# Second input projection: three weight tiles in one piece instead of split, and the first sample's attention four slots later

## What is computed

```python
proj = jnp.einsum('btd,dn->btn', x, w_in)          # x (tokens, 1024), w_in (1024, columns)
q_c, k_c, v_c, g_c, q_d, k_d, v_d, a_d, g_d = jnp.split(proj, ...)
# samples: 32 pages of 128 cached rows, 8 heads of 64
z = jnp.einsum('bqhd,bkhd->bhqk', qblk, kf) + bf
log_1mb = jnp.where(causal, jax.nn.log_sigmoid(-z), 0.0)
suffix = lax.cumsum(log_1mb, axis=3, reverse=True)
excl = jnp.concatenate([suffix[..., 1:], jnp.zeros_like(suffix[..., :1])], axis=-1)
att = jnp.where(causal, jnp.exp(jax.nn.log_sigmoid(z) + excl), 0.0)
out = jnp.einsum('bhqk,bkhd->bqhd', att, vf)
```

## Time and profile before

| | us |
|---|---|
| median of 3 runs (lowest to highest) | 4384.45 (4380.44 to 4393.51) |
| the profiled execution, its span | 4400.05, 4398.3 |
| PE busy in the span | 3311.5 (75%) |
| DVE, ACT, POOL busy | 2270.3, 1114.8, 876.9 |
| mean granted TensorE clock | 0.867 of 2.4 GHz |

### The profile page before, as it was taken

One profiled execution on the slowest core, in us unless ns is written; L12 is line 12 of the kernel. 1 busy time (PEld: TensorE's weight loads), 2 busy tenths in 40 slices (PEclk: granted clock), 3 DMA queues, 4 the chain that ended last, 5 costly groups with the idle time before them and its releaser, 6 DMA issues. The chain is left out here.

```text
span 4398.3 us, 80744 instructions
## 1 busy us (share of the span) xinstructions
PE 3311.5 (75%) x31326; PEld 2805.6 (64%) x31326; DVE 2270.3 (52%) x3271; ACT 1114.8 (25%) x2113; POOL 876.9 (20%) x724
## 2 busy tenths in 40 slices
PE   8799998999922068746968999979777877254279
PEld 6799998999921057725857777758555555153167
DVE  2456664444444942225554766421387777412466
ACT  0045552222213011121000110100276767210400
POOL 4100002222202411002222111022254555000021
PEclk9999999999966566678988999989899999676689
DMA  3445552232223000044554999843301100332343
GB/s 134 149 130 151 149 152 60 47 60 48 47 83 145 0 5 0 0 166 164 177 183 154 325 318 335 281 153 96 102 1 49 49 11 1 132 77 65 129 167 107
DMA packets 435128, 506.29 MB, mean 115 GB/s; under 512 B 179825, under 2 KB 328962, under 8 KB 423370
## 3 DMA queue, kind: packets, MB, share of 16 engines
q1 hardware_dynamic: 318202, 350.22, 25.6%
q10 hardware_dynamic: 116048, 147.59, 10.0%
q0 software_dynamic: 576, 4.21, 0.2%
HBM read 355.56 MB, written 146.36 MB: 114 GB/s over the span
## 5 line engine op out<-in xcount | busy, mean ns | idle before, releaser
L2235 POOL TENSOR_TENSOR sp_att<-sp_beta,sp_left 128x512 f32<-128x512 f32 (+3 forms) x320 | 303.7, 957 | 316.1 <-DVE sp_left L2191 307.2
L102 PE MATMUL po_acc<-po_x_high,po_w_low 128*128 128x412 f32 (+1 forms) x840 | 310.1, 369 | 54.5 <-POOL po_w_low L95 35.7
L102 PE MATMUL pe_acc<-pe_x_high,pe_w_low 128*128 128x412 f32 (+1 forms) x840 | 304.4, 362 | 22.0 <-DVE pe_x_low L95 13.7
L1094 POOL TENSOR_TENSOR rc_ct<-rc_m,rc_lev 128x256 f32<-128x256 f32 x160 | 123.3, 806 | 923.5 <-DVE rc_m L1050 923.5
L103 PE MATMUL po_acc<-po_x_low,po_w_high 128*128 128x412 f32 (+1 forms) x840 | 301.5, 359 | 0.0
L104 PE MATMUL po_acc<-po_x_high,po_w_high 128*128 128x412 f32 (+1 forms) x840 | 300.2, 357 | 0.0
L104 PE MATMUL pe_acc<-pe_x_high,pe_w_high 128*128 128x412 f32 (+1 forms) x840 | 295.3, 352 | 0.0
L103 PE MATMUL pe_acc<-pe_x_low,pe_w_high 128*128 128x412 f32 (+1 forms) x840 | 295.1, 351 | 0.0
L2191 DVE TENSOR_TENSOR_SCAN sp_left<-sp_z,sp_left,sp_zero 128x512 f32<-128x512 f32 x192 | 235.6, 1268 | 97.5 <-ACT sp_z L2135 97.5
L2081 PE MATMUL sp_t<-sp_id,sp_att 128*128 128x128 f32 x1088 | 180.3, 288 | 121.2 <-DVE sp_aT L2197 112.5
L2081 PEld LDWEIGHTS sp_t<-sp_id,sp_att 128*128 128x128 f32 x1088 | 118.2, 144 | 186.1 <-issue 182.6
(11 more groups left out here) (442 smaller groups left out, 8146.2 us busy)
## 6 DMA issues: line engine op xcount, KB each, us to landing
po_work<-in_cache_k SPq DMA_DIRECT2D x256, 256.0 KB, 4.9
po_work<-in_cache_v ACTq DMA_DIRECT2D x256, 256.0 KB, 4.8
scratch_ops<-pe_work SPq DMA_DIRECT2D x160, 128.0 KB, 2.1
rc_opx<-scratch_ops SPq DMA_DIRECT2D x32, 640.0 KB, 8.0
out_z<-pe_o SPq DMA_DIRECT2D x84, 206.0 KB, 2.7
out_z<-po_o ACTq DMA_DIRECT2D x84, 206.0 KB, 4.3
po_w<-in_w_o ACTq DMA_DIRECT2D x23, 512.0 KB, 5.2
pe_w<-in_w_e SPq DMA_DIRECT2D x21, 512.0 KB, 6.3
```

Of the source, the lines that this page charges most:

```text
L102: pe.matmul(out, ll, rh, start=start, stop=False)
L1094: pool.tensor_tensor(ct[q][:, n], m4[q][:, :, 0, :], every(lev[:, n + 1, :]), ALU.mult).then_inc(sem["ct"][q], 1)
L2235: pool.tensor_tensor(att[h][:, n % 3, 0:w], be[h][:, n % 4, 0:w], left[h][tile(n) % 2][:, at + 1:at + 1 + w], ALU.mult).then_inc(at_ok[h], 1)
```

## The change

The order of the groups is changed: tiles 0 and 1 come whole (slots 0 to 9), then block 4 of tile 2 (slot 10), then tile 3 with its last block first (slots 11 to 15), then the other four blocks of tile 2 (slots 16 to 19). From slot 20 on the tiles are as before. There are 22 groups instead of 24. START is 16 instead of 12, and with it every step of the samples stands four slots later; Q_AT follows from the new order and is 13 instead of 9.

```diff
-ODD_GROUPS = ([(0, range(NBLK))] + [(n, [NBLK - 1]) for n in (1, 2, 3)] + [(n, range(NBLK - 1)) for n in (1, 2, 3)]
-              + [(n, range(NBLK)) for n in range(4, 21)])
+ODD_GROUPS = ([(0, range(NBLK)), (1, range(NBLK)), (2, [NBLK - 1]), (3, [NBLK - 1, *range(NBLK - 1)]),
+               (2, range(NBLK - 1))] + [(n, range(NBLK)) for n in range(4, 21)])
@@
-        START, PER = 12, 10
+        START, PER = 16, 10
```

## The result

The changed kernel takes 4371.98 us (median of 22 runs, 4339.45 to 4387.84), the kernel before in the same comparison 4383.03 (22 runs, 4363.24 to 4437.59). The ratio is 0.9961 with a 95% interval of 0.9942 to 0.9980: 0.4% faster, 9 to 25 us. A second comparison of the same changed kernel gave 0.9944 (0.9918 to 0.9971), 13 to 36 us. A copy of the kernel before gave 1.0033 (1.0004 to 1.0061) against itself, so these intervals are too narrow, and the runs alone hardly tell a gain of 0.4% from chance.

A forecast was written before the change was run, and what follows sets the result against it. PE's own idle time was taken to bound the stage, chiefly waits for split weights and attention weights. Terms of 5.2 + 5.4 + 5 + 9.3 = 24.9 us less took 4384.45 to 4360, range 4346 to 4377.

The forecast's parts named there:

- The early slots: PE from slot 5 to slot 20: fewer waits for split weights, so slot 20 starts 23.1 us earlier.
- START: All sample steps on PE and ACT stand four slots later, 17.9 us, so the first exponential comes 5.2 us earlier.
- my margin of 4.6 us: Ahead of ACT's first exponential: DVE's bias for the first sample ends 4.6 us before ACT wants it.
- The attention weights: PE's seven waits for `po_att`, now in slots without a weight request: 5.4 us less, ends 0 and 15.0.
- only the slots: Rival, 25 in 100: the wait for `po_att` doesn't shrink, a V page or bandwidth being late; 14.5 us left, 4370.
- The clock: Behind the `po_att` waits: shorter idle time loses the clock less often, 5 us less, ends 0 and 12.
- The tail: From slot 101 to the stage's end, four V groups following slot 104: 9.3 us shorter, 7.2 to 10.4.
- The sum: All terms together: 5.2 (first sample) + 5.4 + 5 + 9.3 = 24.9 us less.
- the likeliest case: The forecast itself with all its terms, 53 in 100: 4360 us, own range 4349 to 4368.
- The slower rival, K's pages behind: DVE's wait for K: it decides from 3.9 us a pair on, 4407 us at 4.1; 5 in 100.

The follow-up runs named there:

- START 15: The changed kernel with START at 15 instead of 16: stage 666.5 us, ratio 0.9980 to the kernel before.
- order-only kernel: The kernel before with the new order of the groups, START left at 12: stage 659.9 us, ratio 0.9969 to the kernel before.
- request-last kernel: The kernel before with ACT's weight request moved behind its page loads and the samples' steps in the same slot: stage 655.3 us, ratio 0.9960.
- START 17: The changed kernel with START at 17 instead of 16: stage 653.7 us, ratio 0.9970 to the kernel before.
- chain first: The changed kernel with ACT's V page loads moved behind the samples' steps of the same slot: stage 621.0 us, ratio 0.9878 to the kernel before.
- both further edits: The changed kernel with tile 3's weights requested behind slot 8 and V page loads behind the samples' steps: stage 611.7 and 612.9 us, ratios 0.9855 and 0.9917.

## Why the prediction was right

The predicted 4360 and the range of 4346 to 4377 hold the measured 4371.98, and the direction is right; in size the runs give 17 us (9 to 25) by the ratio where 24.9 was forecast, and 25 (13 to 36) in the second comparison. The stage itself gave more than forecast, 28.7 and 27.4. That the sum came so near is partly luck, as the term of the clock was too small and that of the tail too large.

*The early slots.* Forecast 23.1, measured 102.9 - 80.0 = 22.9 in the first pair of profiles and 104.6 - 81.7 = 22.9 in the second. The wait at slot 11 was 8.4 us and the slot behind it 6.4.

*START.* Forecast 17.9, measured 17.9 (from slot 20 to the first exponential 32.5 in place of 14.6). The first sample was ready: ACT did not wait for DVE at the exponential. But my margin of 4.6 us was taken to the wrong instruction. ACT's logarithm waited 3.4 us for DVE's clamp (2.9 before), and START 15 and the order-only kernel showed what happens when the margin goes.

*The attention weights.* Forecast 5.4, measured 15.0 - 10.1 = 4.9 and 15.6 - 10.2 = 5.4. The request-last kernel shows the mechanism alone, START 17 shows it come back (but for its last sample, which has no request), chain first shows that the rest of the wait was ACT's queue too. The rival "only the slots" fell.

*The clock.* Forecast 5, this was the term sized too small. From the first exponential on, the stretch that was 472.7 us long up to slot 101 is 457.9 up to slot 104's end: 14.8 less, of which 4.9 are waits. The other 9.9 are mostly the clock, which stood at 1.2 GHz for 27 us of this stretch before and 10 after, worth 8.5 us at half speed. With waits of 2.1 us each the clock fell behind 5 of 7, three times over (before twice, START 17); with 1.4 to 1.5 us behind 2 to 4 of 7 in six profiles, 15 of 42. In the three profiles without these waits there was no fall at their places. The exception is the order-only kernel, 3 falls at 2.2 us each, but these were longer: 24 us at the lower clock in all. Wait by wait, 18 of the 26 that took 1.9 to 2.6 us brought a fall and 15 of the 44 that took 1.3 to 1.8: a longer wait brought it more often. The rule of the Trainium skill (TensorE: Matmul & The Clock Gate, the section on the oscillation in real kernels), by which gaps this short cost nothing, disagrees with these traces; it would have left out 8.5 of the 14.8 us that this stretch gave.

*The tail.* Forecast 9.3 with ends of 7.2 and 10.4, measured 24.6 - 17.4 = 7.2. The loads were issued when expected, but the second group, whose pages I had counted as there, had to wait as well (1.67 us), and from the second of these waits on PE was at the lower clock: two groups and the heads took 0.8 us more each, where I had allowed half a microsecond in all.

*The sum.* 0 for the start of the stage up to slot 5 (measured 1.7, 0.1 in the second pair), 5.2 (5.0), 10.4 (14.8), 9.3 (7.2): 24.9 forecast, 28.7 measured. The own range of the likeliest case, 4349 to 4368, is narrower than what its bounds add up to: all low ends give 9.8 us less and all high ends 42.6, from 4342 to 4375.

The slower rival, K's pages behind, didn't come: DVE's waits for K were 76.2 us in 60 waits against 70.8 in 59. DVE's slack halved, though (22.7 and 28.3 us in the two profiles). In the kernel with both further edits it is 7.0 and 9.1, and ACT's logarithm waits for DVE's clamp five times, 13.5 and 15.0 us in all, so DVE is likely the next limit; no run tests that.

## What to carry to other kernels

An engine that both issues transfers and computes is a queue: what stands ahead of the short step that another engine waits for costs its issue time each period, and changing the order within the slot (no instruction more or less) was worth 17 to 21 us for the page loads in the changed kernel and 12 to 14 for the weight request in the one before; the new schedule as a whole brought 28. When something is moved out of one slot, look at what it now stands ahead of. A margin between a producer and a fixed slot must be counted up to the last step of the chain, with all the producer puts between the steps. And where a stage's gain is 25 us in runs that scatter by 40, compare the stage in several profiles before believing the median.

## What the runs showed of the hardware

The lower clock can cost more than the idle time that brings it. A wait of 1.9 to 2.6 us, followed by V and head matmuls, brought 3.4 to 10.2 us at 1.2 GHz in 18 of 26 cases in four profiles. Three waits of 2.1 to 2.2 us, at samples 2, 4 and 5 of the kernel before, brought 6.8 us each, 3.4 us lost at half speed; in that kernel's samples' stretch as a whole 27.3 us at the lower clock cost 13.6 us, beside 15.0 us of waits. In the order-only kernel the clock fell during the wait of 18.2 us and stayed low for 20.5 us, 14.4 of them within the wait. Eight page loads issued back to back take ACT 7.9 us and start some 1.06 us apart, as four do in 3.5 us, and the last pages of the stage, with K's loads long over, still kept PE waiting up to 4.62 us.
